# Output projection and its norm issued inside the mixer stage, one sub-tile at a time

## What is computed

```python
u = rmsnorm(h, norm_mix_w)
proj = u @ w_in                                  # 1024 -> 2816
o_hg = rmsnorm(hgrn2_chunkwise(q, k, v, log_f)) * silu(hg)     # recurrent, chunks of 64
o_att = sliding_window_attention_with_sinks(...)               # blocks of 128
mix = concatenate([o_hg, o_att])
h = h + mix @ w_out                              # output projection
v = rmsnorm(h, norm_ffn_w)                       # norm behind it
gate = causal_depthwise_conv(v @ w_gate)
h = h + (silu(gate) * (v @ w_up)) @ w_down       # 1024 -> 2816 -> 1024
return rmsnorm(h, final_norm_w)
```

## Time and profile before

| | us |
|---|---|
| median of 2 runs | 1987.07 (1987.0 to 1987.14) |
| the profiled execution | 1983.4 |
| its span, slowest core (core 4) | 1981.8 (cores 1969.8 to 1981.8) |
| PE busy | 1602.0 (81%) |
| DVE busy | 984.6 (50%) |
| ACT busy | 782.5 (39%) |
| POOL busy | 625.7 (32%) |

### The profile page before, as it was taken

One profiled execution on the slowest core, in us unless ns is written; L12 is line 12 of the kernel. 1 busy time (PEld: TensorE's weight loads), 2 busy tenths in 40 slices (PEclk: granted clock), 3 DMA queues, 4 the chain that ended last, 5 costly groups with the idle time before them and its releaser, 6 DMA issues.

```text
span 1981.8 us, 27976 instructions; the slowest of 8 cores (1969.8 to 1981.8 us)
## 1 busy us (share of the span) xinstructions
PE 1602.0 (81%) x8374; PEld 739.6 (37%) x8534; DVE 984.6 (50%) x1526; ACT 782.5 (39%) x1313; POOL 625.7 (32%) x1238
## 2 busy tenths in 40 slices
PE   0757877769888798878988789787988879787897
PEld 0333333334434343433434344333443434343343
DVE  1354454546545465454645556454654546445452
ACT  1443334334443344433453334433444434443330
POOL 2102431136411362133611255113631236212342
PEclk9868998989988898998999999898998989998999
DMA  9743995963435544464435544355443554455346
GB/s 225 145 110 52 219 239 113 244 218 128 160 103 154 190 137 129 139 197 155 140 115 165 186 148 150 102 165 191 133 155 116 164 179 137 127 150 180 127 145 218
DMA packets 84675, 309.71 MB, mean 156 GB/s; under 512 B 9264, under 2 KB 9392, under 8 KB 84400
## 3 DMA queue, kind: packets, MB, share of 16 engines
q0 software_dynamic: 68352, 247.50, 45.0%
q1 hardware_dynamic: 16176, 60.42, 8.3%
HBM read 291.10 MB, written 41.94 MB: 168 GB/s over the span
## 4 chain that ended last, share of the span: by engine, by line
PE 51%; DVE 14%; issue 12%; ACT 10%; DMA 8%; POOL 4%; DVEq 0%; ACTq 0%; POOLq 0%; SPq 0%
PE ps L619 13%; PE ps L680 10%; PE ps L683 9%; PE ps L439 4%; PE ps L657 4%; DMA wsl<-w_up 3%; PE ps L487 3%; DVE ubf L399 2%; ACT ubf L396 2%; DMA wscr<-wsl 2%; PE ps L409 2%; DVE PT L569 2%; DMA xt<-x 1%; ACT PT L568 1%; DVE fA L453 1%
## 5 line engine op out<-in xcount | busy, mean ns | idle before, releaser
L305 POOL DMA_DIRECT2D wsl<-wscr x439 | 238.0, 542 | 703.8 <-PE ps L439 239.1
L619 PE MATMUL ps<-wsl,actT 128*128 128x512 bf16 x1356 | 336.1, 391 | 43.9 <-DVE xt L626 32.2
L683 PE MATMUL ps<-vT,wsl 128*128 128x512 bf16 x1404 | 337.1, 383 | 29.6 <-DMA wsl<-w_up 14.0
L680 PE MATMUL ps<-vT,wsl 128*128 128x512 bf16 x1348 | 335.6, 389 | 15.9 <-ACT vT L411 13.1
L439 PE MATMUL ps<-uT,wsl 128*128 128x512 bf16 x1070 | 279.6, 420 | 75.8 <-DVE fA L452 61.8
L696 DVE SCALAR_TENSOR_TENSOR cA<-Gb,csts,cA 128x512 f32<-128x512 f32 x176 | 132.0, 750 | 202.8 <-POOL cA L691 201.0
L689 ACT ACTIVATE Gb<-ps 128x512 f32<-128x512 f32 x176 | 105.0, 597 | 286.6 <-PE ps L680 246.5
L683 PEld LDWEIGHTS ps<-vT,wsl 128*128 128x128 bf16 x1408 | 137.0, 99 | 208.9 <-issue 55.0
L619 PEld LDWEIGHTS ps<-wsl,actT 128*128 128x128 bf16 x1408 | 130.0, 100 | 209.3 <-issue 87.7
L680 PEld LDWEIGHTS ps<-vT,wsl 128*128 128x128 bf16 x1408 | 138.6, 100 | 177.3 <-issue 25.3
L439 PEld LDWEIGHTS ps<-uT,wsl 128*128 128x128 bf16 x1088 | 112.0, 105 | 240.9 <-issue 140.5
(11 more groups left out here) (114 smaller groups left out, 1881.2 us busy)
## 6 DMA issues: line engine op xcount, KB each, us to landing
wsl<-wscr POOLq DMA_DIRECT2D x409, 512.0 KB, 4.5
wscr<-wsl SPq DMA_DIRECT2D x47, 512.0 KB, 11.4
xt<-x SPq DMA_DIRECT2D x8, 2048.0 KB, 7.9
out<-xt SPq DMA_DIRECT2D x32, 512.0 KB, 3.3
wsl<-wscr POOLq DMA_DIRECT2D x30, 256.0 KB, 3.9
wsl<-w_in POOLq DMA_DIRECT2D x11, 512.0 KB, 13.4
wsl<-w_gate POOLq DMA_DIRECT2D x11, 512.0 KB, 15.9
wsl<-w_up POOLq DMA_DIRECT2D x11, 512.0 KB, 17.1
```

Source lines behind the costliest of these rows:

```text
L305: S.op("pool", (lambda e, dst=dst, scr=scr: e.dma_start(out=dst, in_=scr)), [f"scr{sid}"], [f"w{slot}"], dma=f"w{slot}")
L619: S.op("pe", lambda e, fc=fc, c=c, s=s, bank=bank, w=w: e.matmul(ps[bank][:, 0:512], lhsT=actT[:, c, s * P:(s + 1) * P], rhs=w[:, fc, :], ...
L680: S.op("pe", lambda e, kc=kc: e.matmul(ps[bg][:, 0:T], lhsT=wg_t[:, kc, m * P:(m + 1) * P], rhs=vT[:, kc, :], start=(kc == 0), stop=(kc == ...
L683: S.op("pe", lambda e, kc=kc: e.matmul(ps[bu][:, 0:T], lhsT=wu_t[:, kc, m * P:(m + 1) * P], rhs=vT[:, kc, :], start=(kc == 0), stop=(kc == ...
```

## The change

`outproj_norm2` becomes a generator (`outproj_gen`) that may take sub-tile `s` as soon as the mixer has finished it (`mix_done`). It is run as the second half of a new `tail_gen`, which first does the down projection of the step before with **two** of its turns for each turn of the mixer, then `final` and the load of the next `x`, and then the output projections. `tail_gen` gets its turn after the mixer's, so everything in it is recorded between one turn of the mixer and the next. The output projection now uses banks 0 and 3 for every sub-tile, and `norm_b` bank 0. The order in which `inproj` cycles through the banks is changed too.

```diff
-            b = [0, 1, 2, 3, 4, 5, 6, 7][dense_bank[0] % 8]
+            b = [0, 1, 4, 5, 6, 7, 2, 3][dense_bank[0] % 8]
...
-        def mixer_gen(st):
+        def mixer_gen(st, mix_done):
             for s in range(NSUB):
+                if s > 0:
+                    mix_done[0] = s
...
+            mix_done[0] = NSUB
...
-        def outproj_norm2(st):
+        def outproj_gen(st, mix_done):
             xb = st % 2
-            wt = [w_next()] + [w_next(hold=True) for _ in range(3)]
+            wt = None
             for s in range(NSUB):
+                while mix_done[0] <= s:
+                    yield
+                if wt is None:
+                    wt = [w_next()] + [w_next(hold=True) for _ in range(3)]
                 for nh in range(2):
-                    bank = 2 + (2 * s + nh) % 4
+                    bank = (0, 3)[nh]
...
                 norm_a(xb, 1, s)
+                yield
                 if s > 0:
-                    norm_b(s - 1, vT, UT2)
-            norm_b(NSUB - 1, vT, UT2)
+                    norm_b(s - 1, vT, UT2, bank=0)
+            yield
+            norm_b(NSUB - 1, vT, UT2, bank=0)
+
+        def tail_gen(st, mix_done):
+            if st > 0:
+                for i, _ in enumerate(down_gen(st - 1)):
+                    if i % 2 == 1:
+                        yield
+                final(st - 1)
+                if x_state["next"] < nst and x_state["next"] == st + 1:
+                    x_load(x_state["next"])
+                    x_state["next"] += 1
+            yield from outproj_gen(st, mix_done)
...
-            gens = [mixer_gen(st)]
-            if st > 0:
-                gens.append(down_gen(st - 1))
-            interleave(gens)
-            if st > 0:
-                final(st - 1)
...
-            outproj_norm2(st)
+            mix_done = [0]
+            interleave([mixer_gen(st, mix_done), tail_gen(st, mix_done)])
```

More of the change, by code:

```diff
@@ L400, in norm_a, with norm_b @@
                  [f"xt{xb}s{s}", sk, "nw3"], [ubk])
-        def norm_b(s, dstT, dkeys):
+        def norm_b(s, dstT, dkeys, bank=None):
             ub = ubf[s % 2]
             ubk = f"ubf{s % 2}"
-            bank = tr_bank[0] % 2
-            tr_bank[0] += 1
+            if bank is None:
+                bank = tr_bank[0] % 2
+                tr_bank[0] += 1
             pv = psb(bank).rearrange("p (c t) -> p c t", t=P)
@@ L661, in outproj_norm2 @@
                 norm_a(xb, 1, s)
+                yield
                 if s > 0:
-                    norm_b(s - 1, vT, UT2)
-            norm_b(NSUB - 1, vT, UT2)
+                    norm_b(s - 1, vT, UT2, bank=0)
+            yield
+            norm_b(NSUB - 1, vT, UT2, bank=0)
+        x_state = {"next": 1}
+        def tail_gen(st, mix_done):
[8 more added lines that the diff above has]
+            yield from outproj_gen(st, mix_done)
         def ffn_gateup(st):
@@ L736, in build_nc @@
         norm_T(0, 0, uT, UT1)
-        x_next = 1
         if nst > 1:
             x_load(1)
-            x_next = 2
+            x_state["next"] = 2
         for st in range(nst):
@@ L743, in build_nc @@
             inproj(st)
-            gens = [mixer_gen(st)]
-            if st > 0:
-                gens.append(down_gen(st - 1))
-            interleave(gens)
-            if st > 0:
-                final(st - 1)
-                if x_next < nst and x_next == st + 1:
-                    x_load(x_next)
-                    x_next += 1
-            outproj_norm2(st)
+            mix_done = [0]
+            interleave([mixer_gen(st, mix_done), tail_gen(st, mix_done)])
             if st == 0:
```

## The result

The changed kernel takes 2128.15 us (median of 9 runs) where the kernel before took 1987.94 (8 runs beside it): ratio 1.0706, 95% interval 1.0694 to 1.0718, so 7% slower, 140 us.

What follows compares the result with a forecast made beforehand. The prediction took PE's order and waits to bound the kernel (PE busy 81%). Seven steps at 13.5 us net loss (31.7 less 18.2), 94.5, plus 16.6 in step 0, made 111 more: 2096 us, range 2045 to 2130.

Steps and rivals of the forecast that it cites:

- The walk: Second half, from last down adds to gate, laid out in DVE's order: 64.9 us against 33.2, loss 31.7 a step.
- The first half: Down projection at double rate beside the mixer's first 24 turns: 50.0 us against 68.2, gain 18.2 a step.
- the sum: Terms added up: 50.0 us for mixer with down projection, 64.9 to the gate; net loss 13.5 a step over 7 steps.
- change of round: In mixer with down projection, PE waits 1.6 us for a bank at only one of three such changes.
- Step 0: Mixer alone, output matmuls and norms ahead of three sub-tiles' masks: end at 200.4 against 183.8, loss 16.6 us.
- The gaps of 2.5 us ahead of L399: Sign of being right: DVE gaps of 2.5 us between `final` and the fourth sub-tile's end, state updates directly behind.
- PE's clock: Sign of being right: clock 0.5 to 0.6 between `final` and the fourth sub-tile's end, PE waiting for DVE.
- The two bursts on the path: 16 output matmuls before the fourth sub-tile's masks and the last 16, each 5.4 us instead of 3.6.
- the bounds: Bursts 3.6 to 6.9 us, first half 48 to 53, bank 7 wait none to 1.2; together 2055 to 2130.
- the wait for bank 7: Mixer's first transposes wait for value projection's adds: start 1.2 us later each step; without it total moves by -8.
- rival 3: Slower: the ring bounds the first half, 58 us instead of 50 at 199 GB/s, total 2150; chance 0.08.
- Rival 1 and 2: Faster, norm waits on DVE filled, 1920, chance 0.05; no change, only first norm hurts, 1965 to 1985, chance 0.08.

Runs made afterwards that it cites:

- e9: Changed kernel with all four norms recorded behind the mixer, output matmuls and adds still woven in; ratio 1.0523, 2091 us.
- e4: Kernel before with one edit: two turns of the down projection per mixer turn, output projection still behind the mixer; ratio 1.0322, 2051 us.
- e1: Changed kernel with the old bank order in the input projection; ratio 1.0665.
- e3: Changed kernel with one turn of the down projection per mixer turn instead of two; ratio 1.0189, 2025 us.
- e8: Changed kernel with waiting bursts of output matmuls recorded one turn later and their norm's last DVE instruction two turns after; ratio 1.0508, 2088 us.
- b2: Kernel before, output projection reordered in place: last norm between its sub-tiles, each norm's last DVE instruction behind the next adds; ratio 0.9669, 1921 us.

## Why the prediction was right, and what it missed

**The walk.** Against the timeline of the changed kernel in step 2 (T = 0 is the start of the last down adds, 674.93):

```profile
674.93 1.29 DVE L630 TENSOR_TENSOR xt<-ps,xt 128x512 f32<-128x512 f32 x2 [0.88 <-PE ps L623]
...
683.39 1.48 DVE L668 TENSOR_TENSOR xt<-ps,xt 128x512 f32<-128x512 f32 x2
684.23 4.43 PE L665 MATMUL ps<-wsl,mixT 128*128 128x512 bf16 x10 [4.84 <-DVE xt L668]
...
688.61 0.68 DVE L529 TENSOR_TENSOR stmp<-ps,Sst 128x512 f32<-128x512 f32 x1
...
694.88 1.28 DVE L399 SCALAR_TENSOR_TENSOR ubf<-xt,stat,nw3s 128x1024 bf16<-128x1024 f32 x1 [2.51 <-POOL stat L398]
696.08 0.68 DVE L529 TENSOR_TENSOR stmp<-ps,Sst 128x512 f32<-128x512 f32 x1
...
703.26 0.58 PE L510 MATMUL ps<-ident,ktT 128*128 128x128 bf16 x4 [0.97 <-DVE t L550]
...
705.56 5.55 PE L665 MATMUL ps<-wsl,mixT 128*128 128x512 bf16 x15 [0.33 <-issue]
```

```profile
727.40 5.08 PE L665 MATMUL ps<-wsl,mixT 128*128 128x512 bf16 x16 [1.94 <-DVE mixT L551]
...
739.62 1.87 PE L703 MATMUL ps<-vT,wsl 128*128 128x512 bf16 x4 [1.26 <-ACT vT L412]
```

| event, T in us | predicted | measured |
|---|---|---|
| `final` off DVE | 8.5 | 8.5 |
| first state update | 13.8 | 13.7 |
| second state update | 21.3 | 21.2 |
| fourth sub-tile begins | 28.4 | 28.3 |
| its burst of output matmuls | 30.1 | 30.6 |
| last burst | 52.0 | 52.5 |
| gate | 64.9 | 64.7 |

The order of DVE, laid beside durations from rows of the kernel before, gave each of these to 0.5 us. The first half was 50.2 us from the first transposes to T = 0, and 1.1 of wait ahead of it: 51.3, where the sum had 50.0 with that wait. The sum gave one change of round a wait of 1.6; all three had one, 2.5 in all. Step 0 lost 15.9, predicted 16.6. The gaps of 2.5 us ahead of L399 are as forecast. PE's clock is 0.66 from the end of `final` to the last burst (683.39 to 727.40), above the 0.5 to 0.6 that was forecast.

The two bursts on the path took 5.6 and 5.1 us in step 2, near the 5.4 from the row. Over steps 1 to 7 the first of them took 4.2 to 5.6 and the last 5.0 to 6.3, and step 0's last 6.6. So none ran wholly at half clock (6.9 in the bounds), but the last came near it in some steps, and 5.4 was an average rather than a fixed price. The burst off the path (684.23 to 690.39, two rows of the timeline) took 6.2.

**Too small by 32 us.** 2096 stood on record, 2128 was measured, 2 us inside the upper end of the range. Three terms:
- *The step that I took as typical was the slowest of steps 2 to 7.* Step 2 is 101.4 before; they have a mean of 100.1. Afterwards all take about 114.6. The loss a step was 14.5, not 13.5: 6 us over these six steps. That step 2 comes out to the tenth (114.9 afterwards, 50.0 + 64.9 in the sum) is in part luck: the sum's 50.0 holds the wait for bank 7, and the measured step does not.
- *Step 1.* Multiplied by 7 as if it were like the others. It lost 25.3 us, 12 more than the sum had: rival 3 (the ring as the bound of the first half) was given 0.08 for all steps and was true in this one, where the tiles come from float32. Its first half fell only from 70.4 to 63.4 us, far outside the bounds of 48 to 53. So it is in part luck that the total still lies in the range. The DMA share of step 1 in the kernel before would have told:

```profile
338.60:390.00 51.40, 40.95 (x280) 19.73 (x284) 27.12 (x59) 18.29 (x33) 7.93 (x15) 0.97 0.98 211
```

- *Outside the stage.* The wait for bank 7 (1.1 a step, as priced, but counted in the first half) lies ahead of the stage of the table: 9 us over 8 steps. The gate stage is some 0.7 a step longer, 82.6 against 82.0 over steps 1 to 6. On average 11.7 of its matmuls instead of 9.7 are at the lower clock (631 ns instead of 379 in the records), which would make an estimated 0.4 us of it; what makes the rest is not shown.

Rival 1 and 2 needed the norms to run in the mixer's shadow; e9 shows that without them in the mixer's chain a step is still 111.0. Even without the 6.5 us that e9 pays back at the gate it would be some 104.5, so their full removal would not have brought the kernel back to 100.

**Where the 140 us come from**, by experiments: 64 from the double rate (e4), of these 47 in steps 2 to 7 and 19 in step 1; 68 from the weaving with its two banks instead of four (e1 less e4), of these 39 in steps 2 to 7, 16 in step 0 and 7 in step 1; 8 from the new bank order. The parts by step do not add up exactly, since the other stages move by some us too. In steps 1 to 7 the weaving exists only because of the double rate (e3). The split of the weaving between burst and norm is not a sum: norm 14 and burst 15 us alone, 39 together, and 36 for the norms' removal with a payback of 6.5 us a step at the gate.

What stays open: why e8's steps 2 to 7 stop at 110.8. Their third sub-tile still takes 31.3 us in step 2 (31.8 in the changed kernel, 14.2 in e4, where only the last 11 matmuls of the down projection stand in it): `final` and the first two sub-tiles' adds and norms stand there. How much of that is `final`, and how much the clock, no run separates, since none took `final` out of the mixer without paying elsewhere.

## What to carry to other kernels

Where engines work through queues in a fixed order, write down the order of the engine that everything goes through (DVE here) and lay the durations along it; a chain of four short instructions over three engines costs its whole latency (5.2 us for 2.8 of DVE's work, with the adds ahead of it) to all that is queued behind, and it matters less which stage it is moved to than what is recorded between its parts. Filler work that a latency-bound stage needs should be spread over all of it: giving it out at double rate in the first half gained 17 us there and cost 24 behind (e4, step 2). And the first pass over weights that are converted on the way in is a case of its own; cost it apart.

## What the runs showed of the hardware

The small POOL instruction that raises to the power -0.5 (one number per partition) takes 0.56 us in the norms of the output projection, but 1.44 where it starts beside DVE's 128 x 1024 instruction of the last norm (L730 before, L753 after: there 548 to 1442 ns, median 1438 over 32). In the changed kernel's step 2:

```profile
678.47 1.28 DVE L753 SCALAR_TENSOR_TENSOR xt<-xt,stat,nw3s 128x1024 f32<-128x1024 f32 x1 [0.58 <-POOL stat L752]
678.72 1.44 POOL L752 TENSOR_TENSOR stat<-stat,cns 128x1 f32<-128x1 f32 x1
```

It ends 0.4 us after the DVE instruction does, and the next DVE instruction waits 0.58 us for it, so the last norm has a period of 1.87 us a sub-tile instead of 1.28. In b2, where the same instruction does not start behind such a DVE instruction, all 28 took 547 to 568 ns; this holds too for the 15 that had a DVE instruction of the same form start 0.14 us or more after them. The Trainium skill, page "SBUF — State Buffer", section "Who interferes with whom", says that a DVE instruction with two inputs in SBUF contends with a GpSimd instruction that reads SBUF, and that the port pair which they share is an exclusive lock. The trace agrees with it (1.44 us beside such an instruction, 0.56 without); no run here was made to test it.
